# First attention: the probabilities times their reciprocal sums on GpSimd in place of VectorE, and one wait of the mixing stage at another place

## The reference

```
s = einsum('bnqhgd,bnkhd->bnhgqk', qb, kw) * HEAD_DIM ** -0.5
s = where(mask, s - slopes * dist, -inf)
m = max(max(s, axis=-1), sink)
p = exp(s - m)
denom = sum(p, axis=-1) + exp(sink - m)
o = einsum('bnhgqk,bnkhd->bnqhgd', p / denom, vw)
return o.reshape(B, T, ATTN_Q_DIM) @ w_out
```

```
qk = silu(centred_dwconv(qk, conv_w))
```

## Time and profile before

| what | value |
|---|---|
| median of 3 runs | 847.94 us (847.42 to 848.12) |
| the profiled execution, whole | 849.05 us |
| its span, first to last instruction | 846.9 us |
| TensorE matmul busy | 833.6 us (98%) |
| VectorE busy | 579.5 us (68%) |
| ScalarE busy | 438.0 us (52%) |
| GpSimd busy | 56.3 us (7%) |
| mean TensorE clock granted | 0.998 of full |
| share of TensorE in the chain that ended last | 90% |

### The profile page before, as it was taken

One profiled execution on the slowest core, in us unless ns is written; L12 is line 12 of the kernel. 1 busy time (PEld: TensorE's weight loads), 2 busy tenths in 40 slices (PEclk: granted clock), 3 DMA queues, 4 the chain that ended last, 5 costly groups with the idle time before them and its releaser, 6 DMA issues.

```text
span 846.9 us, 12751 instructions
## 1 busy us (share of the span) xinstructions
PE 833.6 (98%) x5026; PEld 727.8 (86%) x5026; DVE 579.5 (68%) x614; ACT 438.0 (52%) x600; POOL 56.3 (7%) x121
## 2 busy tenths in 40 slices
PE   8999999999999999999999999999999999999996
PEld 8877988888888799989888888999867988888885
DVE  5797656665758689886866666677587476666663
ACT  6666544344435688665544444456664454444431
POOL 2100000000000213410000000012000000000000
PEclk9999999999999999999999999999999999999999
DMA  9735355655564485365766665444524276555611
GB/s 332 269 142 179 121 184 168 214 182 185 177 232 153 167 282 198 102 193 147 251 196 198 198 198 198 143 144 149 168 64 155 94 248 198 189 181 185 193 46 50
DMA packets 92359, 149.78 MB, mean 177 GB/s; under 512 B 4540, under 2 KB 71628, under 8 KB 91808
## 3 DMA queue, kind: packets, MB, share of 16 engines
q1 hardware_dynamic: 90608, 143.90, 50.9%
q0 software_dynamic: 1424, 5.07, 1.8%
q10 hardware_dynamic: 288, 0.27, 0.1%
HBM read 148.15 MB, written 1.06 MB: 176 GB/s over the span
## 4 chain that ended last, share of the span: by engine, by line
PE 90%; DVE 3%; ACT 3%; DMA 2%; issue 1%; SPq 1%; DVEq 0%; POOLq 0%; POOL 0%; ACTq 0%
PE bank L1971 19%; PE bank L1972 19%; PE bank L1973 19%; PE bank L1999 17%; PE bank L2002 9%; DMA w_raw<-laid_swa_w_in_blocks 2%; ACT arena L1178 1%; PE bank L2055 1%; ACT w_hi L701 1%; PE bank L2369 1%; PE bank L2161 1%; PE bank L2180 1%; DVE w_lo L1232 1%; DVE arena L1905 1%; PE bank L2678 0%
## 5 line engine op out<-in xcount | busy, mean ns | idle before, releaser
L1232 DVE TENSOR_TENSOR w_lo<-w_raw,w_hi 128x2048 fp32r<-128x2048 f32 (+2 forms) x126 | 282.6, 2249 | 65.5 <-ACT w_hi L701 65.5
L701 ACT ACTIVATE w_hi<-w_raw 128x2048 fp32r<-128x2048 f32 (+1 forms) x128 | 239.4, 1878 | 54.1 <-PE bank L1973 40.4
L1999 PE MATMUL bank<-xT,w_hi 128*128 128x512 f32 x640 | 159.4, 391 | 0.0
L1999 PEld LDWEIGHTS bank<-xT,w_hi 128*128 128x128 f32 x640 | 117.1, 188 | 22.3
L1971 PE MATMUL bank<-w_hi,ff_hi 128*128 128x512 f32 x344 | 134.5, 391 | 0.0
L1972 PE MATMUL bank<-w_lo,ff_hi 128*128 128x512 f32 x344 | 134.3, 390 | 0.0
L1973 PE MATMUL bank<-w_hi,ff_lo 128*128 128x512 f32 x344 | 133.9, 389 | 0.0
L1971 PE MATMUL bank<-xT,w_hi 128*128 128x256 f32 (+1 forms) x428 | 123.3, 288 | 1.3 <-ACT arena L960 0.8
L1972 PE MATMUL bank<-xT,w_hi 128*128 128x256 f32 (+1 forms) x428 | 121.0, 283 | 0.0
L1973 PE MATMUL bank<-xT,w_lo 128*128 128x256 f32 (+1 forms) x428 | 121.0, 283 | 0.0
L2002 PEld LDWEIGHTS bank<-xT,w_lo 128*128 128x128 f32 x640 | 87.3, 190 | 6.2
(11 more groups left out here) (274 smaller groups left out, 913.7 us busy)
## 6 DMA issues: line engine op xcount, KB each, us to landing
w_raw<-in_ffn_w SPq DMA_DIRECT2D x64, 1024.0 KB, 5.3
w_raw<-in_ffn_w_gate_up SPq DMA_DIRECT2D x22, 1024.0 KB, 5.1
w_raw<-in_ab_w_in SPq DMA_DIRECT2D x12, 1024.0 KB, 6.9
w_raw<-in_ffn_w_down SPq DMA_DIRECT2D x11, 1024.0 KB, 5.3
w_raw<-in_swa_w_out SPq DMA_DIRECT2D x4, 1024.0 KB, 6.8
w_raw<-in_ab_w_out SPq DMA_DIRECT2D x4, 1024.0 KB, 4.9
w_raw<-in_c_w_out SPq DMA_DIRECT2D x4, 1024.0 KB, 5.1
w_raw<-laid_swa_w_in_blocks SPq DMA_DIRECT2D x3, 1024.0 KB, 14.5
```

Of the source, the lines that this page charges most:

```text
L701: act.activation(view(w_hi, ch), view(w_raw, ch), ACT.Copy).then_inc(S["hi_done"], 1)
L1232: dve.tensor_tensor(view(w_lo, ch), view(w_raw, ch), view(w_hi, ch).bitcast(F32), ALU.subtract).then_inc(S["lo_done"], 1)
L1999: pe.matmul(bank[b + f], hi[:, k, f * P:(f + 1) * P], xT[:, k].rearrange("p s t c -> p (s t c)"), start=k == 0, stop=False)
```

## The change

The product moves from VectorE's `swa_normalised` to a new GpSimd function `swa_shares`, which waits for a new semaphore `swa_rden_ready` that VectorE sets behind its reciprocals. `swa_reciprocals` stands wherever `swa_normalised` stood. GpSimd does the two halves of group 0 ahead of its wait for the exponentials and its copy of the sinks of group 3, and the six others behind that copy, ahead of the load of the gain. The signal `swa_normed`, on which the transposes wait, is set by GpSimd. In the mixing stage TensorE's wait for `conv_begun` 4 moves behind projections 9 and 10. The semaphore `swap_ready` is gone, with its wait on TensorE. The lists of semaphore names change with these; the rest of the diff is:

```diff
 @block.gpsimd
+            def swa_shares(g, half):
+                h = 4 * g + 2 * half
+                pool.wait_ge(S["swa_rden_ready"], 2 * g + half + 1)
+                p = swa_s[:, g % 3, 2 * half:2 * half + 2, 1:1 + SWA_COLS].rearrange("p j (b k) -> p j b k", b=3)
+                pool.tensor_tensor(p, p, swa_rden[:, h:h + 2, :].unsqueeze(3).broadcast_to([P, 2, 3, P]),
+                                   ALU.mult).then_inc(S["swa_normed"], 1)
...
             for g in range(4):
                 if g == 3:
+                    for half in range(2):
+                        swa_shares(0, half)
                     pool.wait_ge(S["swa_probs"], 8)
                 pool.tensor_copy(swa_s[:, g % 3, :, 0:SWA_COLS + 2:SWA_COLS + 1],
                                  sinks[:, 4 * g:4 * g + 4].unsqueeze(2).broadcast_to([P, 4, 2])).then_inc(S["swa_sinks_ready"], 1)
+            for g in range(1, 4):
+                for half in range(2):
+                    swa_shares(g, half)
             pool.wait_ge(S["gain_loaded"], 16)
             load_gain(2)
             norm((1, 0), (1, 1))
 @block.vector
             for a in range(2):
                 dve.tensor_copy(swap.rearrange("p (j a i) -> p j a i", a=2, i=HALF)[:, :, a],
-                                ident.rearrange("p (j a i) -> p j a i", a=2, i=HALF)[:, :, 1 - a]).then_inc(S["swap_ready"], 1)
+                                ident.rearrange("p (j a i) -> p j a i", a=2, i=HALF)[:, :, 1 - a])
...
-            def swa_normalised(g, half):
+            def swa_reciprocals(g, half):
                 h = 4 * g + 2 * half
                 dve.wait_ge(S["swa_probs"], 8 * g + 4 * half + 4)
                 dve.reciprocal(swa_rden[:, h:h + 2, 0:2], swa_sum[:, :, h:h + 2].rearrange("p t h -> p h t"))
-                step(dve.reciprocal(swa_rden[:, h:h + 2, 2:3], swa_sum[:, 1, h:h + 2].unsqueeze(2)))
-                p = swa_s[:, g % 3, 2 * half:2 * half + 2, 1:1 + SWA_COLS].rearrange("p j (b k) -> p j b k", b=3)
-                dve.tensor_tensor(p, p, swa_rden[:, h:h + 2, :].unsqueeze(3).broadcast_to([P, 2, 3, P]),
-                                  ALU.mult).then_inc(S["swa_normed"], 1)
+                dve.reciprocal(swa_rden[:, h:h + 2, 2:3], swa_sum[:, 1, h:h + 2].unsqueeze(2)).then_inc(S["swa_rden_ready"], 1)
...
             swa_bias(1, 0)
-            swa_normalised(0, 0)
-            swa_normalised(0, 1)
+            swa_reciprocals(0, 0)
+            swa_reciprocals(0, 1)
             swa_bias(1, 1)
             queries(2)
             swa_maxima(1)
             swa_bias(2, 0)
             low_upto(o[0].index + 1)
-            swa_normalised(1, 0)
+            swa_reciprocals(1, 0)
             swa_bias(2, 1)
             queries(3)
-            swa_normalised(1, 1)
+            swa_reciprocals(1, 1)
             swa_operand(0)
             swa_bias(3, 0)
             swa_maxima(2)
             low_upto(o[1].index + 1)
-            swa_normalised(2, 0)
+            swa_reciprocals(2, 0)
             swa_bias(3, 1)
             swa_operand(1)
             swa_maxima(3)
-            swa_normalised(2, 1)
-            swa_normalised(3, 0)
-            swa_normalised(3, 1)
+            swa_reciprocals(2, 1)
+            swa_reciprocals(3, 0)
+            swa_reciprocals(3, 1)
             low_upto(o[2].index + 1)
             swa_operand(2)
 @block.tensor
-            pe.wait_ge(S["conv_begun"], 4)
             pe.wait_ge(S["vb_ready"], 2)
             projection(9)
             projection(10)
+            pe.wait_ge(S["conv_begun"], 4)
             scores_T(0)
             scores_T(1)
...
             pe.wait_ge(S["c_k_ready"], 3)
-            pe.wait_ge(S["swap_ready"], 2)
             swapped(0)
```

More of the change, by code:

```diff
@@ L320, in build @@
             "warm_ready gain_cols_loaded "
-            "head1_loaded head2_loaded swa_rb_ready swa_R_psum swap_ready "
+            "head1_loaded head2_loaded swa_rb_ready swa_R_psum "
             "ff1_gs ff1_us ff2_sum ff1_sg ff1_h ff1_t ff1_hi ff1_lo ff2_t ff2_relu ff2_h ff2_hi ff2_lo "
             "swa_q_ready swa_k_ready swa_v_ready swa_scores swa_biased swa_nmax swa_probs swa_pt_psum "
-            "swa_pt_ready swa_sinks_ready swa_normed swa_o_psum swa_oh_ready swa_ol_ready "
+            "swa_pt_ready swa_sinks_ready swa_rden_ready swa_normed swa_o_psum swa_oh_ready swa_ol_ready "
             "g_raw_ready g4_loaded g_abs_ready g_ln_ready g_rows_ready g_cols_psum g_cols_ready g_em_ready "
```

## The result

The changed kernel takes 848.87 us (median of 22 runs, 848.29 to 849.57), the kernel before 847.71 us (22 runs on the same chips, 846.80 to 848.39): ratio 1.0015, 95% interval 1.0010 to 1.0021. It is slower by 1.2 us: beyond doubt slower, but under the 0.2% that I had called telling. The forecast was 850.8 us in a range of 848.2 to 852.2. The time lies in the range, on its low side, between the forecast and rival B.

The account below looks back on a forecast made before the run. TensorE, busy 833.6 of 846.9 us, was taken to bound the kernel. The attention's total delay of +3.7 and the moved wait's -0.83 gave +2.9 us on the median 847.94: 850.8 us, range 848.2 to 852.2.

Parts of the forecast that it names:

- rival B: First attention's end: no costly blocking, last product goes first or overlaps the split; +0.6 us, 848.5 us; chance 0.16.
- the last product and the split: First attention's end: VectorE's two-SBUF-input weight split goes first and blocks GpSimd's last product, which then runs 72.65 to 74.46.
- The moved wait, -0.83: Mixing stage: projection 9 no longer waits for ScalarE's fourth convolution start, so begins 0.83 us earlier; bounds -1.1 and 0.
- The slack of 1.5 us before scores_T(0): Mixing stage: scores_T(0), now behind the moved wait, starts at 336.2; ScalarE's silu ends at 334.68, so nothing queues.
- Rival D: Mixing stage: the moved wait returns nothing, as VectorE's and ScalarE's chain sets the end; +3.7, 851.6 us; chance 0.06.
- The product, 1.81 us: First attention: GpSimd's price for each 128x768 product, between bounds of 0.96 and 2.2 us, with 0.2 us fixed.
- T(0,0) +0.57: First attention, transpose 0 of group 0: waits for GpSimd's product, starts at 43.93 instead of 43.36 us.
- T(1,1) +0.85: First attention, transpose 1 of group 1: late scores and GpSimd's product move it to 56.8 from 55.96 us, total delay.
- T(2,0) +1.16: First attention, transpose 0 of group 2: later split, then GpSimd's product; starts at 63.26 instead of 62.10 us.
- T(3,1) +3.7: First attention, transpose 1 of group 3: last product stands behind the weight split; starts at 74.56 instead of 70.9 us, total delay.
- A: The main forecast: slower through the blocked last product, 850.8 us, own range 849.9 to 852.3; chance 0.72.
- C: First attention: GpSimd's product costs no more than VectorE's 0.96 us, the 0.65 us idle goes; -1.5, 846.5 us; chance 0.06.

Follow-up runs that it names:

- the best run with GpSimd: Changed kernel with products (0,0), (2,0), (3,1) back on VectorE and reciprocals of (1,1) ahead of the bias of (2,1) and queries 3: 846.27 us, ratio 0.9984.

## Why the prediction was right, and where it wasn't

- **That the change loses, through the last product and the split.** Right, and shown from four sides: the loss goes with a wait, with another engine, with another kind of instruction and with a later issue. That the split goes first was my estimate, as no row of the kernel before shows it: the split, which needs no signal, started at 68.60 us and the product at 68.77, and these 0.17 us were enough. In these runs the product took 1.47 us beside an instruction with one SBUF input and 3.44 beside the split with two, and whichever of product and split started first kept its own time: the split 2.27 us with the product at 3.44, the product 1.47 with the split at 3.41.
- **The moved wait, -0.83.** Right: -0.9 by the rows and by the run of its own. The slack of 1.5 us before scores_T(0) was enough. Rival D falls.
- **The product, 1.81 us.** Too dear: 1.47. The fixed part of 0.2 us was about right (0.18 by the line through two sizes); the price of an element, taken from the earlier trace rows, was 2.1 ns where the line has 1.67.
- **T(0,0) +0.57, T(1,1) +0.85, T(2,0) +1.16.** Measured +0.24, +0.10, +0.50. These terms were mis-sized, and mostly by the price of the product, which is 0.34 us less. It enters T(0,0) once. T(1,1) came at 56.06 and not at 56.8: the first product's 0.34 us, handed on through the scores of (2,1), and the second product's 0.34. T(2,0) came at 62.56 and not at 63.26: 0.34 is its own product, and the split ahead of it started at 57.78 + 0.75 = 58.53, not at 58.78. I had let that split be held up by the scores, but VectorE, rid of the product of (1,1), no longer reaches the bias ahead of it late.
- **T(3,1) +3.7.** Measured +2.3, at 73.01 and not at 74.56. I let the exponentials of group 3 end 0.85 us later; with T(1,1) nearly in place the last reciprocals end where they did (68.69 + 0.75 = 69.44, and 69.45 before). From their end to T(3,1) I had 74.56 - 70.3 = 4.3 us, it was 3.6. Of the difference 0.34 is the product itself; the largest part of the rest is that the split didn't wait for product (3,0), which was over at 68.48.
- **The chance.** I gave 0.72 to slower by over 0.2% and the change came to 0.15%: the case was A, but under the lower end of A's own range (849.9), which a product of 1.5 us was to give; that end still carried the too late reciprocals. So the mechanism was right and its size wasn't: the sum said +2.9 us and the change is +1.2. That the time lies in the stated range is in part luck, as the range was drawn down to 848.2 for rival B's sake. Rival B named nearly the right time for a wrong reason: without the block the kernel takes 847.3 to 847.6 us, not 848.5. C is excluded, as the product would have had to take 1.3 us or less and still wait its turn.

## What to carry to other kernels

Before work moves from VectorE to GpSimd, look at what stands right behind the hand-over in VectorE's queue. Here it was an instruction with two SBUF inputs, issued 0.17 us before GpSimd could start, and the product took 3.44 us instead of 1.47; behind an instruction with one SBUF input it took 1.47. With six small instructions between the two it took 1.47 as well and the split 3.41, and with a wait the product took 1.48 and the split 2.29.

Give GpSimd the products with slack behind them and keep on VectorE those for which TensorE waits. What that brings beyond the moved wait is small in this kernel and not clear of noise: the best run with GpSimd measured 846.27 us (ratio 0.9974 to 0.9993), the moved wait alone 846.87 (0.9982 to 1.0000), and by the rows T(3,0) stands 35.41 us behind the second score product against 35.70.

A term that is priced too dear enters a timetable once for each step in which it stands: 0.34 us of one product had become 0.7 us at T(1,1), and by way of that step I had the last reciprocals 0.86 us too late.

## What the runs showed of the hardware that I had not expected

GpSimd's product costs 1.67 ns for an element and 0.18 us fixed by a line through 128x384 and 128x768, and at 128x768 it takes 1.47 us whether one operand is broadcast or both are full. The two blocks agree in size: the eighth product is 1.97 us longer than the others (3.44 against 1.47), and 68.60 + 2.27 - 68.77 = 2.10 us of the split lay ahead of it when it started; the mirrored block adds 1.13 us to the split (3.41 against 2.28), where 68.42 + 1.47 - 68.63 = 1.26 us of the product lay ahead. So in both directions the longer row shows about 0.13 us less than what was left of the other.
